# Taking the norm's root out of the expert layer's inputs in a two-block transformer kernel

## The reference, cut to what matters

```python
xn2 = rms_norm(h, norm2_g)                    # h * rsqrt(mean(h*h) + eps) * g
q = (xn2 @ wq).reshape(tokens, 8 heads, 2, 128)
s = einsum('chpd,hpkd->chpk', q, subkeys)     # 16 score rows of 128 keys for each token
# for each head: top 16 of each half, the top 16 of their 256 sums, softmax over these: g, eidx
hid = einsum('cd,chkd->chk', xn2, u_table[eidx])
a = gelu(hid) * g
out = einsum('chk,chkd->cd', a, v_table[eidx])   # added to h, then a last norm
```

## Time and profile before

| | |
|---|---|
| time, median of 3 runs | 2270.02 us (2269.95 to 2271.81) |
| the profiled execution's own time | 2269.04 us |
| its span, first to last instruction | 2267.2 us |
| TensorE busy | 2210.5 us (97%) |
| VectorE busy | 1304.5 us (58%) |
| ScalarE busy | 902.4 us (40%) |
| GpSimd busy | 1244.4 us (55%) |

### The profile page before, as it was taken

How to read it: one execution, slowest core, us unless ns; L and a number is a source line. 1 busy time by engine, 2 the same in 40 slices (tenths; PEclk the granted TensorE clock), 3 DMA queues, 4 the chain that set the end, 5 groups by cost and what they waited for, 6 DMA issues and landing times.

```text
span 2267.2 us, 29807 instructions
## 1 busy us (share of the span) xinstructions
PE 2210.5 (97%) x9694; PEld 1736.1 (77%) x9694; DVE 1304.5 (58%) x2401; ACT 902.4 (40%) x1429; POOL 1244.4 (55%) x824
## 2 busy tenths in 40 slices
PE   8999999999999998999999999999999999999998
PEld 5666665777777776788888888888887888888886
DVE  5454332225643685797676665222223988888887
ACT  4565544335544554434323333222222433333333
POOL 3432022244434332268888888888886655555553
PEclk9999999999999999999999999999999999999999
DMA  7664233325423221245666666666656999999996
GB/s 244 200 212 150 79 89 125 90 92 171 149 75 103 76 85 47 93 94 90 147 144 148 140 147 145 144 148 127 113 105 190 351 325 358 349 356 350 353 356 241
DMA packets 240050, 396.96 MB, mean 175 GB/s; under 512 B 87992, under 2 KB 162744, under 8 KB 239712
## 3 DMA queue, kind: packets, MB, share of 16 engines
q1 hardware_dynamic: 161088, 328.48, 44.6%
q0 software_dynamic: 78880, 67.50, 14.9%
HBM read 330.60 MB, written 61.01 MB: 173 GB/s over the span
## 4 chain that ended last, share of the span: by engine, by line
PE 58%; DVE 2%; ACT 0%; DMA 0%; issue 0%; SPq 0%; DVEq 0%; ACTq 0%
PE bank L1474 30%; PE bank L1485 23%; PE bank L1230 4%; PE bank L1457 0%; ACT staged L1525 0%; DMA tail<-gates 0%; DVE u_split L2278 0%; DVE low L1966 0%; DVE tail L2210 0%; DVE tail L2245 0%; DVE tail L2243 0%; DVE tail L2246 0%; DVE tail L2189 0%; DVE staged L2192 0%; DVE tail L2199 0%
## 5 line engine op out<-in xcount | busy, mean ns | idle before, releaser
L1107 POOL DMA_INDIRECT gates<-low x384 | 627.9, 1635 | 140.3 <-issue 116.8
L1474 PE MATMUL bank<-h_high,u_tiles_split 128*128 128x512 f32 x2048 | 630.9, 389 | 2.2 <-DVE u_tiles_split L2177 2.2
L1075 POOL TENSOR_TENSOR u_split<-blocks,u_split 128x1024 fp32r<-128x1024 f32 (+1 forms) x102 | 245.2, 2404 | 586.7 <-ACT u_split L1629 558.0
L1230 PE MATMUL bank<-h_high,u_split 128*128 128x512 f32 x1664 | 540.5, 400 | 10.8 <-POOL u_split L1075 6.8
L1485 PE MATMUL bank<-v_split,a_split 128*128 128x512 f32 x2286 | 520.2, 390 | 2.8 <-DVE a_split L2317 2.8
L1485 PEld LDWEIGHTS bank<-v_split,a_split 128*128 128x128 f32 x2286 | 430.1, 188 | 92.9 <-DVE v_split L2314 3.1
L1474 PEld LDWEIGHTS bank<-h_high,u_tiles_split 128*128 128x128 f32 x2048 | 384.6, 188 | 81.9 <-issue 2.4
L1474 PE MATMUL bank<-h_low,u_tiles_split 128*128 128x512 f32 x1024 | 398.6, 389 | 0.0
L1230 PEld LDWEIGHTS bank<-h_high,u_split 128*128 128x128 f32 x1664 | 313.7, 189 | 86.6 <-issue 21.3
L2177 DVE TENSOR_TENSOR u_tiles_split<-tail,u_tiles_split 128x1024 fp32r<-128x1024 f32 x128 | 157.1, 1228 | 361.5 <-ACT u_tiles_split L1816 360.6
L1230 PE MATMUL bank<-h_low,u_split 128*128 128x512 f32 (+1 forms) x704 | 274.4, 390 | 0.0
(11 more groups left out here) (232 smaller groups left out, 2360.9 us busy)
## 6 DMA issues: line engine op xcount, KB each, us to landing
tail<-in_uT SPq DMA_DIRECT2D x128, 512.0 KB, 3.8
tail<-in_v SPq DMA_DIRECT2D x128, 512.0 KB, 5.4
gates<-blocks SPq DMA_DIRECT2D x32, 768.0 KB, 5.8
tail<-gates SPq DMA_DIRECT2D x128, 192.0 KB, 5.6
kept_hidden<-tail SPq DMA_DIRECT2D x96, 192.0 KB, 1.9
tail<-kept_hidden SPq DMA_DIRECT2D x96, 192.0 KB, 5.7
blocks<-in_r SPq DMA_DIRECT2D x24, 512.0 KB, 4.0
blocks<-in_conv SPq DMA_DIRECT2D x16, 512.0 KB, 4.4
```

Source lines behind the costliest of these rows:

```text
L1075: nc.gpsimd.tensor_tensor(flat(u, 1)[:, 0:n], ring[:, loads[0] % NW, 0:n], flat(u, 0)[:, 0:n].bitcast(F32), ALU.subtract).then_inc(s_wlo, 1)
L1107: nc.gpsimd.indirect_dma_start(gate_elements, bass.IndirectOffsetOnAxis(ap=expert_no[tb][:, k:k + 1], axis=0), expert_gate[tb][:, k:k + 1] ...
L1230: last = mm(ps[0:m, :], flat(u, part)[:, k * m:(k + 1) * m], x, start=(k == 0 and j == 0), stop=(k == nk - 1 and j == 2))
L1474: last = mm(bank[slot % 2][:, :], U4[:, slot, w, k, :], x[:, k, :], start=(k == 0 and x is hh and w == 0), stop=(k == KD - 1 and w == 1))
```

## The change

The roots are no longer multiplied into the normalised tiles of this norm (key `h2`).

- As soon as a residual tile f is added, VectorE writes its high part as tile times gain (`early_high`) and then its low part (`early_low`), within the output projection's steps. Normalised tiles and the step `high_h` are gone for this norm.
- The first half (12 matmuls) of the first query projection stands ahead of the norm's own matmuls. The fillers are left out for this norm. The order of the first queries and score blocks is new.
- The roots are made twice: as rows along the tokens (`root_rows`), and, by eight products with two columns of ones, as one column for each block of 128 tokens (`rinv`).
- The scores get the root when they leave their bank: four ScalarE activations of 128 tokens, each with its column as scale, in place of one copy.
- The hidden sums get it on VectorE (`scale_hidden`): a product of the bank with the root rows, written to SBUF. Gelu then works in place there and waits for that, and so does TensorE before it writes the bank again. In VectorE's order the scaling of tile e - 3 stands right ahead of the low part of tile e.
- The buffer of raw expert weights and one of the value weights lie elsewhere.

```diff
+        STEPS.append(("early_high", "h2", f))
+        STEPS.append(("early_low", "h2", f))
         STEPS.append(("square", "h2", f))
         if 0 < f < KD - 1:
             STEPS.append(("sum", "h2", f))
+    part(len(PROJ), 0, 4)
     STEPS.append(("norm", "h2"))
-    STEPS.append(("high_h", "h2"))
-    side_by_side("wq")
-    part(len(PROJ), 0, 4)
+    STEPS.append(("first_channels",))
+    tile("wq", 0, KD, P)
+    part(len(PROJ), 0, 2)
     STEPS.append(("keys", 0))
-    for i in range(2, 2 * PEER_HEADS):
-        if i > 2:
-            tile("wq", i, KD, P)
-        STEPS.append(("keys", i - 1))
-        if i == 2:
-            tile("wq", i, KD, P)
+    for i in range(1, 2 * PEER_HEADS):
+        tile("wq", i, KD, P)
+        if i > 1:
+            STEPS.append(("keys", i - 1))
     STEPS.append(("keys", 2 * PEER_HEADS - 1))
...
-        UR = rt(0, 4 * 1024, 4)
+        UR = region(HH, 4 * 1024, 4)
...
-        V2 = [place("v_split0", TAIL + 4096, [2, 2, D], F32R), place("v_split1", HH, [2, 2, D], F32R)]
+        V2 = [place("v_split0", TAIL + 4096, [2, 2, D], F32R), place("v_split1", HH + 4096, [2, 2, D], F32R)]
...
+                    early = {"wq": "h2"}.get(kind)
...
-                        for j, (part, x) in enumerate(((0, high), (0, x_low[:, t, :]), (1, high))):
+                        low = x_low[:, t, :]
+                        if early:
+                            high, low = early_high(early, t), early_low(early, t)
+                            if kind == "wq" and i == 0:
+                                pe.wait_ge(s_early_low, early_no("h2", t))
+                        for j, (part, x) in enumerate(((0, high), (0, low), (1, high))):
...
+                    if key in ("h2", ):
+                        for tb in range(TB):
+                            to, tokens = ax[(i + 1) % 2][:, 2 * tb:2 * tb + 2], slice(tb * P, (tb + 1) * P)
+                            mm(to, rs[:, tokens], ones[:, 0:2], start=True, stop=False)
+                            last = mm(to, sq[:, j % NQ, tokens], ones[:, 0:2], start=False, stop=True)
+                        last.then_inc(s_tok, 1)
...
-                    keep_busy(i, 3)
+                    if key not in EARLY_PHASES:
+                        keep_busy(i, 3)
...
             def hidden(e, slot):
 
                 pe.wait_ge(s_ulo, e + 1)
-                at_least(pe, s_gelu, e - 1)
+                at_least(pe, s_hs, e - 1)
...
-                    for w, x in ((0, hh), (0, hl), (1, hh)):
-                        last = mm(bank[slot % 2][:, :], U4[:, slot, w, k, :], x[:, k, :],
-                                  start=(k == 0 and x is hh and w == 0), stop=(k == KD - 1 and w == 1))
+                    for j, (w, x) in enumerate(((0, early_high), (0, early_low), (1, early_high))):
+                        last = mm(bank[slot % 2][:, :], U4[:, slot, w, k, :], x("h2", k),
+                                  start=(k == 0 and j == 0), stop=(k == KD - 1 and j == 2))
                 last.then_inc(s_hid, 1)
...
                 A(r, r, ACT.Exp, scale=-0.5).then_inc(s_rs, 1)
+                if key in ("h2", ):
+                    n = EARLY_PHASES.index(key) - EARLY_PHASES.index("h2")
+                    act.wait_ge(s_tok, n + 1)
+                    A(rinv[:, 0:2 * TB], ax[(i + 1) % 2][:, 0:2 * TB], ACT.Ln, bias=col("eps")).then_inc(s_tokrs, 1)
+                    act.wait_ge(s_tokrs, 2 * n + 1)
+                    A(rinv[:, 0:2 * TB], rinv[:, 0:2 * TB], ACT.Exp, scale=-0.5).then_inc(s_tokrs, 1)
...
+                elif s[0] == "first_channels":
+                    for k in range(TB):
+                        act.wait_ge(s_hx0, TB)
+                        act.wait_ge(s_early_low, early_no("h2", KD - 1))
+                        nc.scalar.copy(xT[:, k, :], bank[3 + k][:, :]).then_inc(s_hxc, 1)
...
-                    nc.scalar.copy(sc[:, i, :], bank[3 + i % 4][:, :]).then_inc(s_qe, 1)
+                    for tb in range(TB):
+                        tokens = slice(tb * P, (tb + 1) * P)
+                        ins = A(sc[:, i, tokens], bank[3 + i % 4][:, tokens], ACT.Identity,
+                                scale=rinv[:, 2 * tb:2 * tb + 1])
+                    ins.then_inc(s_qe, 1)
...
             def kept_tile(e, slot):
-                act.wait_ge(s_hid, e + 1)
-                at_least(act, s_kept[slot], (e - slot) * 8)
-                A(AF[:, slot, :], bank[slot % 2][:, :], ACT.Gelu).then_inc(s_gelu, 1)
+                act.wait_ge(s_hs, e + 1)
+                A(AF[:, slot, :], AF[:, slot, :], ACT.Gelu).then_inc(s_gelu, 1)
                 high_u(e + 3, (slot + 3) % 4)
...
             def on_chip_tile(e):
-                act.wait_ge(s_hid, e + 1)
-                A(on_chip[:, e - NS, :], bank[e % 2][:, :], ACT.Gelu).then_inc(s_gelu, 1)
+                act.wait_ge(s_hs, e + 1)
+                A(on_chip[:, e - NS, :], on_chip[:, e - NS, :], ACT.Gelu).then_inc(s_gelu, 1)
...
-            def norm(key):
+            def early_parts(key, k, low):
+
+                x, g = xT[:, k, :], col({"x": "norm", "x2": "norm1", "h2": "norm2"}[key], k)
+                if not low:
+                    if key == "x":
+                        dve.wait_ge(s_x[k // 2], 16)
+                    else:
+                        dve.wait_ge(s_post, post_no[({"x2": "res", "h2": "res2"}[key], k)])
+                    V.tensor_scalar(early_high(key, k), x, g, None, ALU.mult).then_inc(s_early_high, 1)
+                    return
+                dve.wait_ge(s_early_high, early_no(key, k))
+                V.scalar_tensor_tensor(early_low(key, k), x, g, early_high(key, k).bitcast(F32),
+                                       ALU.mult, ALU.subtract).then_inc(s_early_low, 1)
...
+            def scale_hidden(e, slot):
+
+                dve.wait_ge(s_hid, e + 1)
+                at_least(dve, s_kept[slot], (e - slot) * 8)
+                V.tensor_tensor(AF[:, slot, :], bank[slot % 2][:, :], roots("h2"), ALU.mult).then_inc(s_hs, 1)
+
+            def scale_hidden_on_chip(e):
+
+                dve.wait_ge(s_hid, e + 1)
+                V.tensor_tensor(on_chip[:, e - NS, :], bank[e % 2][:, :], roots("h2"), ALU.mult).then_inc(s_hs, 1)
+
+            def next_low_u(e):
+
+                if e >= 3:
+                    scale_hidden(e - 3, (e - 3) % 4)
+                low_u(e, e % 4)
 
             def sorted_half(i):
...
                     for _ in range(0 if h < EARLY else FIRST_LOWS_AT[i] if h == EARLY else LOWS_AT[i]):
-                        low_u(lows, lows % 4)
+                        next_low_u(lows)
...
-            with dve.Fori(lows // 4, NT // 4) as it:
+            with dve.Fori(lows // 4, NS // 4) as it:
                 for u in range(4):
+                    scale_hidden(it * 4 + (u - 3), (u + 1) % 4)
                     low_u(it * 4 + u, u)
+            for e in range(NS - 3, NT):
+                if e < NS:
+                    scale_hidden(e, e % 4)
+                else:
+                    scale_hidden_on_chip(e)
+                if e + 3 < NT:
+                    low_u(e + 3, (e + 3) % 4)
 
```

More of the change, by code:

```diff
@@ L537, in program @@
         o = HH + 12288
+        root_rows = region(spare_off, T)
         oT = region(o, 12 * T, 12)
@@ L835, in program, with early_high, early_low, early_no @@
         H_NO = {"x": 0, "x2": 1, "h2": 2}
+        EARLY_PHASES = ("h2", )
+        def early_high(key, k):
+            return oh[0][:, k, :]
+        def early_low(key, k):
+            return hl[:, k, :] if key == "h2" else (KA if key == "x" else QA)[:, k, :] if k < 4 else \
+                (oh[1] if key == "x" else KA)[:, k - 4, :]
+        def early_no(key, k):
+            return KD * EARLY_PHASES.index(key) + k + 1
+        scaled_no = {}
+        for s in STEPS:
+            if s[0] == "scaled":
+                scaled_no[s[1]] = len(scaled_no) + 1
+        def wait_evacuated(eng, n):
+            if n in scaled_no:
+                eng.wait_ge(s_scaled, scaled_no[n])
+            else:
+                eng.wait_ge(s_evac, ev(n))
+        def roots(key):
+            return root_rows if key in ("h2",) else rs
         parts0 = {key: sum(n for _, n in PHASES[:i]) for i, (key, _) in enumerate(PHASES)}
@@ L1691, in norm @@
                     act.wait_ge(s_norm, j - 1)
-                r = rs[0:rows, 0:N]
+                r = roots(key)[0:rows, 0:N]
                 if key == "x":
@@ L1799, in _ @@
                         nc.scalar.copy(hh[:, k, :], hT[:, k, :]).then_inc(s_hh, 1)
-                        if s[1] == "h2" and k >= TB:
-                            act.wait_ge(s_hx0, TB)
-                            nc.scalar.copy(xT[:, k - TB, :], bank[3 + k - TB][:, :]).then_inc(s_hxc, 1)
                     if s[1] == "x":
@@ L1933, in norm @@
                 dve.wait_ge(s_rs, j)
-                r = rs[0:rows, 0:N]
-                for k in range(nk):
+                r = roots(key)[0:rows, 0:N]
+                for k in ks or range(nk):
                     if key == "x":
```

(15 more changed lines are left out.)

36 lines of the change are left out of this document (33 added, 3 removed).

## The result

| | changed | before |
|---|---|---|
| median (runs) | 2349.31 us (4: 2346.59 to 2351.98) | 2270.91 us (4: 2269.95 to 2274.48) |
| profiled execution, own time | 2346.75 us | 2269.04 us |
| its span, mean granted clock | 2344.9 us, 0.985 | 2267.2 us, 0.995 |

The ratio is 1.0341, with a 95% interval of 1.0328 to 1.0354. The forecast was 2341 us in a range of 2300 to 2360.

A forecast was written before the change was run, and what follows sets the result against it. TensorE, at 97% of the span, was taken as the bound, losing time only where it waits. Terms -3.5 - 1.0 + 0.9 + 74.2 + 0.7 (later gate loads) = +71.3 us on a 2270.02 median gave 2341, range 2300 to 2360.

The forecast's parts named there:

- The hidden tiles, +74.2 us: Hidden tiles: VectorE's scaling, waits and late transfers make TensorE wait; 9.0 in head 2, 13.7 each in 3-6, 10.4 in 7.
- Block 3.43: Hidden tiles: one "scale, wait for gelu and cast, low part" holds VectorE for 3.43 us, before 1.14.
- pair 8.56: Hidden tiles: two blocks in a row last 8.56 instead of 6.86 us, the second cast waiting for its weights.
- The gap once a head: TensorE stands some 6.9 us at the 9.2 us retrieval stretch between heads, 3.6 behind head 7.
- The smaller waits: Hidden tiles: TensorE also waits 0.9 to 2.3 us at four other places of each head.
- some 70 us of idle time: Expected in the profile: hidden-sum matmuls idle some 70 us, released by VectorE's scaling, in gaps near 7 us once a head.
- The rule on the clock: Five 6.9 us gaps and the 3.6 lower TensorE's clock, 1.8 us each; nothing added; otherwise up to 11 us, 2352.
- The norm, -3.5: Norm's gap: 12 early query matmuls, no fillers or two waits, eight small products at 1.5 us; gain 3.5 us.
- queries -1.0: Query stage: about 1 us of TensorE waits goes, VectorE getting the first scores earlier.
- last key copy +0.9: Last key block: four scaled quarter reads, 1.5 us instead of 0.59, delay the first hidden tile's weight cast by 0.9 us.
- Transfers hidden: Hidden tiles: loads land in time, only 6.9 us per head lost, 37 in all: 2304; hidden or half hidden 0.18.
- No loss: Hidden tiles: the block costs VectorE only its 0.69 us, if held under 2.84 us: 2267; chance 0.07.

The follow-up runs named there:

- experiment 3: Changed kernel with only the load queue reordered: weights of tile e + 4 asked for before the two stores of tile e; 2311.42 us, ratio 1.0172.
- experiment 9: Changed kernel with extra identity products on TensorE ahead of six hidden tiles, to fill the long gaps; 2349.20 us, ratio 1.0331.
- experiment 1: Changed kernel without the scaling of the hidden sums, gelu reading the bank as before, the queries' part kept; 2271.39 us, ratio 0.9996.
- experiment 7: Changed kernel with low parts ahead of scalings, and the two-tile place ahead of the 9.2 us retrieval stretch made two one-tile places; 2268.97 us, ratio 0.9982.
- experiments 2 and 4: Changed kernel with the low part ahead of the scaling of tile e - 2, 2276.51 us; changed kernel with early loads and cast ahead of gelu, 2275.33 us.
- experiment 10: The kernel before, unchanged, run once more for a second trace; 2271.84 us.
- experiment 8: First tile's weight cast moved ahead of the last query's copy: in the kernel of experiment 7, 2267.39 us; in the kernel before, 2268.60 us.

## Why the prediction was right, point by point

**The hidden tiles, +74.2 us.** Right, in mechanism and nearly in size. Block 3.43 forecast, 3.46 in the rows above; pair 8.56, found 8.68; head 79.1, found 79.1 to 79.7 between the ends of the long gaps; the cast's wait for transfers some 35, found 35.2. The gap once a head was forecast at 6.9 us and is 6.51, 6.85 and 6.86 in three heads, 5.0 and 5.3 in two, and 3.5 behind head 7 (3.6). The smaller waits, forecast at 0.9 to 2.3 us in four places of a head, are 0.3 to 2.1 us in three or four. The split of the loss, 37 by the block alone and as much again by transfers, was tested by experiment 3: 38 us fell away with the early loads. From the first hidden to the first output matmul it was +78.4 where +74.9 had been worked out, transition included.

**TensorE idles less than it loses.** I expected some 70 us of idle time; it was 58.7. The stage grew by 78.4 us: 56.0 is idle until scalings, 0.6 the longer wait before the outputs, and in the other 21.8 the profile shows TensorE as running. Only a part of these is the lower clock. A matmul's recorded duration overlaps the next one's start, so each wait is longer, by the distance of starts, than the idle time shown: the 3.52 us at 1476.55, with the clock at 1.00 on both sides, delayed the tile after next by 3.81 us. For 25 waits that is some 7 us (an estimate, 25 x 0.3). At the lower clock the tiles behind the five long gaps took 7.1 to 8.1 us, 9.6 us in all above the 5.57 of the tile behind that gap of 3.52 us, and the stage's first tile 1.5 more.

**The rule on the clock.** The drop of the earlier trace rows came behind the five long gaps, and not behind the sixth, where I had forecast it too:

```profile
1476.55 0.47 PE L1521 MATMUL bank<-o_high,u_tiles_split 128*128 128x512 f32 x1 [3.52 <-DVE tail L2294]
```

Behind it the granted clock was 1.00 for the next 8 us; behind the five it was 0.50 for the next 2 us, with first matmuls of 0.76 to 0.77 us. It also fell once where no drop was forecast, to 0.57 in the 4 us behind a wait of 2.05 us at 1143.06. The Trainium skill ("TensorE: Matmul & The Clock Gate", section "HAM oscillation — how this bites in real kernels") says that every burst behind such a wait starts slow; the trace agrees for five of the six. That this would add 11 us isn't what happened; experiment 9 kept the clock up and gained nothing. The assumption that VectorE's lateness takes it in held, but with less to spare than I thought: the tile behind the gap of 6.85 us took 8.1 us, 2.5 more than at the full clock where I had priced 1.8, and VectorE came to its scaling at 1248.77, 9.14 us behind the scaling at 1239.63 (8.9 forecast), when its last matmul, begun at 1248.35, was just done.

**The norm, -3.5, and queries -1.0, last key copy +0.9.** The sum of -3.6 is what the trace shows to the first hidden matmul: -3.64 (116.05 to 112.41), and 112.35 to 112.41 us in all nine traces that have the change and its order of casts against 116.05 and 116.09. The second half of the first query, forecast for 7.8 us behind the last output projection's copy, began 7.64 us behind it; with the 12 matmuls done ahead of it (2.72 us) that is -3.6. The price for the last key copies was smaller, 2.71 us of gap instead of 2.16, +0.55, and so was the gain in the queries, -0.6. That these two cancel so well in the sum is luck. The eight products of two columns took 1.7 us from start to start (926.58 to 928.29), near the 1.5 that was taken.

**The term that was left out.** That gap's growth cost more than itself. The first row is the changed kernel's, the second that of the kernel before, run again:

```profile
1034.32 0.74 PE L1521 MATMUL bank<-o_high,u_tiles_split 128*128 128x512 f32 x1 [2.71 <-DVE u_tiles_split L2286]
```

```profile
1037.24 0.47 PE L1474 MATMUL bank<-h_high,u_tiles_split 128*128 128x512 f32 x1 [2.17 <-DVE u_tiles_split L2177]
```

Behind 2.71 us the matmuls started at the lower clock (0.50 in the changed kernel's next 2 us), behind 2.16 and 2.17 not (1.00). The prediction had the longer gap, +0.9, but no price for the clock behind it. The price can be read closely, since TensorE never waits inside this stage in five of the kernels. First hidden to first output matmul, less the wait before the latter, is 699.32 - 2.75 = 696.57 us in the kernel before, 698.77 - 2.18 = 696.59 in its second trace, 696.57 and 696.57 with the early cast (1731.35 - 1032.26 - 2.52; 1732.32 - 1030.67 - 5.08), but 700.40 - 2.30 = 698.10 in experiment 1 and 701.81 - 3.65 = 698.16 in experiment 7: 1.5 us. So the queries' part gives 3.7 and takes back 1.5. The remaining 2.2 us are inside the interval of experiment 1 (-3.2 to +1.4 us around its -0.9), which can't tell them from nothing.

**The rivals.** "Transfers hidden" (2304) was made real by experiment 3 and came to 2311. "No loss", which needed a block under 2.84 us, was made real by experiments 2 and 4; it left five gaps of 0.85 us that my rival of 2267 didn't see, because two banks give TensorE no more than two tiles of lead over a stretch of 9.2 us, some 1.2 us each by the distance of starts. With that stretch divided it came to 2269.

**In all,** 2341 by the terms, 2349 in the median. The profiled execution took 2346.75 us where the terms give 2340.3. Of the 6.4 us between them 2.8 lie ahead of the norm, where the kernel before scatters as much, and 3.5 in the hidden stage; 1.5 of these are the clock at its first tile, which the prediction left out, and for the other 2.0 no run shows a cause. The median is 2.6 us above the profiled execution, within the scatter of 2346.6 to 2352.0.

## What to carry to other kernels

Before an operation is put onto an engine with idle time, follow what the next instruction of its queue waits for: if it waits for something that the new operation itself releases, the engine's idle time is no reserve, and the round trip (here gelu, cast, and a transfer asked for behind gelu) goes onto the path. Then look for an order in which each round trip spans other work; here the low part put ahead of the scaling, which then takes the sum of the tile two back instead of three, was worth 73 us, and no work had to go. A ring through several queues sets the pace once its round is longer than a tile: moving one member forward (the cast, without the loads) made it 6.5 us where TensorE needs 5.44, and was worse than moving none.

## What the hardware showed that I had not expected

Ahead of the first hidden tile a wait of 2.16 or 2.17 us left the granted clock as it was in both traces of the kernel before, and behind one of 2.71 us it fell in all nine traces that had it (first matmul 0.56 to 0.77 us instead of 0.47), for 1.5 us where that could be read. But the length of the wait alone doesn't decide. In the changed kernel it fell behind 2.05 us at 1143.06 and not behind 3.52 us at 1476.55. Ahead of the first output matmul it fell behind 2.18 us (experiment 10), 2.75 (before) and 3.34 (changed), and not behind 2.30 (experiment 1), 2.52 (experiment 8, in the kernel before) and 3.44 (experiment 3).

In the stages before the change the same instructions took up to 3.5 us more or less between executions: the last output projection was copied out between 918.6 and 922.1 us in thirteen traces. In the three earliest (918.6 to 919.1) the granted clock was 1.00 from 700 to 720 us, in the ten others (920.0 to 922.1) 0.91, in the kernel before as in the changed one.
